# Convolution split by token halves, with gates and second-half taps inside the early attention

## The chip, the cores and the metric

The kernel runs on one core of one Trainium2 chip. The metric is the device time of one execution in microseconds; the median of three runs is given.

## What is computed

One layer of an encoder block on 1024 tokens with 1024 channels, in float32. Cut to what matters here:

```python
h = x @ w_in + b_in
h_conv = h[..., :1024]; q, k, v = ...          # 512 columns each, 8 heads of 64
g_conv, g_sb = sigmoid(h[..., 2560:3584]), sigmoid(h[..., 3584:4608])
# branch A
a, gate = split(h_conv)
c = a * sigmoid(gate)                           # 512 channels
c = causal_depthwise_conv(c, w_dw, width=31) + b_dw
y_conv = silu(layer_norm(c)) @ w_pw2 + b_pw2
# branch B, strictly causal, per head
z = q k^T / 8
att = exp(log_sigmoid(z) + suffix sums of log_sigmoid(-z))
y_sb = (att @ v) @ w_o
# both
mix = (g_conv * y_conv + g_sb * y_sb) @ w_out + b_out
x = layer_norm(alpha * x + mix)
# expert lookup: 8 heads, 16 of 16384 experts per head and token
y = peer(x)
out = layer_norm(alpha * x + y)
```

The 31 taps reach back 30 tokens, so the two halves of the tokens need only 30 columns of each other.

## The kernel before

The tokens are handled in reverse order, as two halves of 512. The "early" half is brought through attention, mixing and the first layer norm ahead of the expert lookup; attention and mixing of the "late" half run inside the lookup (all that has "late" in its name before the change). The diff touches only what lies ahead of the lookup.

Engines work from queues of their own, each in the order of its code, and wait for each other by semaphores. Stages, in the order of TensorE:

- *Projections.* A loop of four rounds (L601) with four weights a round, each weight 128 columns of `w_in` over all 1024 tokens: 48 matmuls in split precision (`split_products`, L206: high and low parts, three products, L209 to L211). A weight fills PSUM banks 2j and 2j+1, with j its place in the round, and waits until `psum_read[j]` says that the weight before it in these banks was read. The host orders the weights (L1622): conv tile c, its gate, q of c, k of c. ScalarE rounds each weight to its high part (L981), GpSimd subtracts to get the low one (L557, L562), in the memory of the weight; the next load of that place (L431) waits for the weight's matmuls. ScalarE makes the sigmoid of the gate (L1008) and evacuates q and k (L1012, L1016).
- *Convolution* on VectorE, tile by tile over both halves at once: gated input (L1322), 31 taps of 128x1024 (L1328, L1331), each waiting for the last one (`Steps.link`).
- *Values.* 8 blocks (`value_block`, L616), and between them mean and variance over channels as matmuls with a constant (L636, L643). VectorE centres and scales (L1341 to L1348), ScalarE does squares, root and swish (L1032 to L1038) and then evacuates the last four value blocks (L1026).
- *Attention*, 16 units n: four head pairs, and in each four query blocks with 512, 384, 256 and 128 keys. Per unit and head: scores (L662), sigmoids of both signs (L1051, L1054), the scan and the multiply on VectorE (L1356, L1360: the "stick"), transposes (L673), a copy (L1061), the product with the values (L685).
- *Gates and branches*, 8 steps m: weight m is rounded on ScalarE (L1084) and subtracted on VectorE (L1374), two gate groups of 24 matmuls (L712), the two branch products (L718), sigmoids (L1092) and `mix` on VectorE (L1382 to L1388).
- *The first output product* (L739) and its layer norm (L1418 on), queries, scores and the selection of experts, and then the lookup: 1024 gathers (L590), each with a dot product on VectorE (L1486).

## Time and profile before

| | |
|---|---|
| median of 3 runs | 3284.27 us (3281.8 to 3286.63) |
| profiled execution | 3283.15 us |
| its span | 3281.3 us |
| TensorE busy | 2446.8 us |
| VectorE busy | 2297.7 us |
| GpSimd busy | 1326.3 us |
| ScalarE busy | 1159.3 us |
| first matmul | 9.57 us |
| first output product ends | about 491.7 us |

The busy shares are means over stages with different limits. Ahead of the lookup the milestones are read from the order of time; in the lookup, from some 520 us on, the DMA engines are full. In rows, PE is TensorE's matmuls, PEld its weight loads, DVE VectorE, ACT ScalarE, POOL GpSimd. `arena_low` and `arena_high` are two overlays of the whole memory of a partition, so their names do not tell tiles apart; the line does.

### The profile page before, as it was taken

To read this page: it belongs to the slowest core of one execution; us is meant where nothing else is said; L and a number is where in the kernel's file an instruction comes from. 1 tells how busy PE (TensorE), PEld (TensorE's weight loads), DVE (VectorE), ACT (ScalarE), POOL (GpSimd) and SP (SyncE) were. 2 spreads that over 40 slices of the span, in tenths; PEclk is the share of its full clock that TensorE was granted. 3 is DMA by queue.
4 is the path that set the end of the run, shared out by engine and by line. 5 is a ranking of instruction groups with operands and counts; after the bars stand their busy time and mean duration, and the time that the engine had idled before them with its cause. 6 is when DMAs were issued, how large, how long until landed. Compare 5 with 4: busy or idle time off the path is not lost. (4 is left out here: it accounts for less than half of the span.)

```text
span 3281.3 us, 37294 instructions
## 1 busy us (share of the span) xinstructions
PE 2446.8 (75%) x12464; PEld 998.8 (30%) x12464; DVE 2297.7 (70%) x4704; ACT 1159.3 (35%) x3326; POOL 1326.3 (40%) x1197
## 2 busy tenths in 40 slices
PE   8987996778778777769899888885555555555555
PEld 7864653332223333323233332221111111111111
DVE  6986215776668888876667866666777677767775
ACT  3106112333334555533333333333333333333332
POOL 3400003344445544544343344444455445444553
PEclk9998997888888898889999999997777777777777
DMA  3101226999999999999999999999999999999997
GB/s 142 39 0 65 77 104 272 396 413 420 421 420 405 410 409 375 409 420 410 397 397 419 394 409 412 421 419 421 409 421 421 420 398 421 421 421 402 421 421 313
DMA packets 162792, 1163.71 MB, mean 355 GB/s; under 512 B 17857, under 2 KB 17985, under 8 KB 26178
## 3 DMA queue, kind: packets, MB, share of 16 engines
q0 software_dynamic: 147456, 1073.81, 79.7%
q1 hardware_dynamic: 15170, 87.79, 6.8%
q8 instruction: 93, 1.52, 0.2%
q14 instruction: 73, 0.60, 0.0%
HBM read 1157.33 MB, written 4.19 MB: 354 GB/s over the span
## 5 line engine op out<-in xcount | busy, mean ns | idle before, releaser
L809 PE MATMUL ps<-arena_high 64*64 64x512 f32 x8192 | 1275.3, 749 | 724.2 <-ACT arena_high L1163 721.2
L590 POOL DMA_INDIRECT arena_high<-uv_dram,idx_now x1024 | 1201.8, 1174 | 1468.7 <-PE ps L809 1269.4
L1486 DVE SCALAR_TENSOR_TENSOR arena_high<-arena_low,arena_high 128x1024 f32<-128x1024 f32 x1024 | 1237.2, 1224 | 631.4 <-DMA arena_high<-uv_dram,idx_now 620.8
L809 PEld LDWEIGHTS ps<-arena_high 64*64 64x64 f32 x8192 | 308.3, 156 | 1567.7 <-ACT arena_high L1163 1101.6
L1154 ACT ACTIVATE gcol<-hcol 128x2 f32<-128x2 f32 x512 | 103.7, 202 | 1405.8 <-DVE arena_high L1486 1403.7
L1163 ACT ACTIVATE arena_high<-arena_high,wcol 128x64 f32<-128x64 f32 x1024 | 300.4, 340 | 16.7
L1156 ACT ACTIVATE wcol<-gcol,arena_high 128x1 f32<-128x1 f32 x1024 | 245.7, 287 | 16.8
L778 PE MATMUL ps<-arena_low 128*128 128x512 f32 (+1 forms) x512 | 223.5, 580 | 0.0
L1331 DVE SCALAR_TENSOR_TENSOR arena_low<-arena_high,cols,arena_low 128x1024 f32<-128x1024 f32 x120 | 183.9, 1533 | 4.3
L585 POOL CAST idx_now<-arena_high 128x8 uint32<-128x8 f32 x128 | 59.0, 461 | 255.3 <-DVE arena_high L1472 254.7
L211 PE MATMUL ps<-x_hi_bytes,w_bytes 128*128 128x512 f32 x384 | 151.0, 393 | 0.0
L778 PEld LDWEIGHTS ps<-arena_low 128*128 128x128 f32 x512 | 93.9, 194 | 140.9 <-issue 124.3
L881 PE MATMUL ps<-arena_low 128*128 128x512 f32 x256 | 121.8, 620 | 0.0
L1154 ACT ACT_TABLE_LOAD x78 | 100.1, 1283 | 29.4 <-DVE arena_high L1486 28.1
L209 PE MATMUL ps<-x_hi_bytes,w_hi_bytes 128*128 128x512 f32 x256 | 100.8, 394 | 9.6 <-DVE x_lo_bytes L1312 9.6
L210 PE MATMUL ps<-x_lo_bytes,w_hi_bytes 128*128 128x512 f32 x256 | 100.6, 393 | 0.0
L1486 DVE DVE_READ_ACCUMULATOR arena_high<-arena_low,arena_high 128x1 f32 x1024 | 83.8, 82 | 0.0
L1148 ACT ACT_TABLE_LOAD x64 | 82.1, 1283 | 1.1
L211 PEld LDWEIGHTS ps<-x_hi_bytes,w_bytes 128*128 128x128 f32 x384 | 73.0, 190 | 15.5
L562 POOL TENSOR_TENSOR w_bytes<-arena_high,w_hi_bytes 128x1024 fp32r<-128x1024 f32 x12 | 34.8, 2906 | 91.0 <-ACT w_hi_bytes L981 90.9
L881 PEld LDWEIGHTS ps<-arena_low 128*128 128x128 f32 x256 | 47.7, 196 | 76.8 <-issue 76.7
L1522 DVE TENSOR_TENSOR_SCAN arena_low<-arena_low 128x1023 f32<-128x1023 f32 (+3 forms) x32 | 60.4, 1887 | 14.3 <-ACT arena_low L1194 13.9
(169 smaller groups left out, 2476.4 us busy)
## 6 DMA issues: line engine op xcount, KB each, us to landing
arena_low<-slabs_dram SPq DMA_DIRECT2D x21, 1152.0 KB
arena_high<-uv_dram,idx_now POOLq DMA_INDIRECT x1024
arena_high<-w_mix_dram SPq DMA_DIRECT2D x8, 1536.0 KB, 6.8
arena_low<-w_mix_dram SPq DMA_DIRECT2D x8, 1536.0 KB
arena_high<-w_proj_dram SPq DMA_DIRECT2D x16, 512.0 KB, 3.5
arena_high<-xT_dram SPq DMA_DIRECT2D x8, 512.0 KB, 7.7
arena_high<-w_out_dram SPq DMA_DIRECT2D x2, 2048.0 KB, 11.1
arena_high<-x_dram SPq DMA_DIRECT2D x8, 512.0 KB, 7.8
```

What stands on the lines that cost most here:

```text
L209: nc.tensor.matmul(out, w_hi, x_hi, start=first, stop=False)
L210: nc.tensor.matmul(out, w_hi, x_lo, start=False, stop=False)
L211: return nc.tensor.matmul(out, w_lo, x_hi, start=False, stop=last)
L590: pool.indirect_dma_start(out=ring[:, s % RING, :], out_offset=None, in_=uv_d, in_offset=bass.IndirectOffsetOnAxis(ap=idx_now[:, s:s + 1], ...
L778: last = nc.tensor.matmul(ps[:, 4 + half, j0 * P:j1 * P], w[:, k, half * P:(half + 1) * P], x1T[:, j0:j1, k, :], start=(k == 0), stop=(k = ...
L809: last = nc.tensor.matmul(ps[out_rows, bank, :], diag[rows, s % DIAGS, :], ring[rows, s % RING, cs], start=False, stop=False, skip_group_c ...
L881: last = nc.tensor.matmul(ps[:, 4 + g, :], w_mix_late[m % 2][:, o:o + P], xT_late[:, k, :], start=(k == 0), stop=(k == KD - 1))
L1154: steps.link(nc.scalar.activation(gcol[:, s0:s0 + 2], hcol[:, s0:s0 + 2], ACT.Gelu))
L1156: last = nc.scalar.activation(wcol[:, s:s + 1], gcol[:, s:s + 1], ACT.Copy, scale=gates[:, t % (BLK * PH), s:s + 1])
L1163: nc.scalar.activation(diag[:, s % DIAGS, :], ident64, ACT.Copy, scale=wcol[:, s:s + 1]).then_inc(diag_ready, 1)
L1331: ins = nc.vector.scalar_tensor_tensor(out=conv_both(c), in0=halves(conv_in[:, PAD - k:PAD - k + S]), scalar=cols[:, tap + k:tap + k + 1], ...
L1486: last = nc.vector.scalar_tensor_tensor(out=ring[:, s % RING, 0:D], in0=x1[c][:, j, :], scalar=1.0, in1=ring[:, s % RING, 0:D], op0=ALU.mu ...
```

## The change

- The host orders the weights: four pairs of conv tile and gate, then all q, then all k.
- The early half of the convolution is done by VectorE beside the projections, with taps of 128x512. The gated input of the late half is kept for all four tiles in `conv_in_late`. PSUM place 0 or 2 of a conv tile is read by VectorE, after the taps of the tile before.
- Statistics, centring and swish are done for each half apart: those of the early half between value blocks 0 and 3, those of the late half in the branch steps 1 to 4.
- The late half's 124 taps follow the early attention's multiplies, four behind each, and go by turns on two tiles, each waiting for the tap before it on its own tile.
- The gates: one of 16 groups of 24 matmuls per attention unit, ahead of the unit's transposes, with a sigmoid each. Their low parts are subtracted by GpSimd instead of VectorE, their weights are loaded apart from the branches' weights. Branch steps keep the branch products alone. Attention's scores have two PSUM banks instead of four.
- Some loads move: the first half of `w_out` comes when the gates are done, the second when the last mix is done; the x rows and bias rows come earlier.

The diff, cut to its core (moved addresses and new semaphores are left out):

```diff
@@ the queue of loads
+            sp_eng.wait_ge(proj_done, 4 * CC)
+            load_gate(0)
+            sp_eng.wait_ge(var_done, 1)
+            load_gate(1)
             sp_eng.wait_ge(v_done, NB)
...
+            for m in range(2, KD):
+                sp_eng.wait_ge(gates_done, 2 * m - 2)
+                load_gate(m)
...
+            sp_eng.wait_ge(mixed, KD)
             sp_eng.dma_start(w_out_early[1], w_out_d[:, CC:KD, :]).then_inc(wout_in[1], 16)
@@ GpSimd
+            def split_gates(m):
+                for g in range(2):
+                    gs = slice(g * D, (g + 1) * D)
+                    pool.wait_ge(w_rounded, m * 2 + g + 1)
+                    nc.gpsimd.tensor_tensor(w_lo_r[:, m % 2, gs], w_gate[:, m % 2, gs], w_hi_r[:, m % 2, gs].bitcast(F32),
+                                            ALU.subtract).then_inc(w_split, 1)
@@ TensorE
+            value_block(0)
+            pe.wait_ge(conv_done, CC)
+            conv_mean(1, 4)
+            value_block(1)
+            value_block(2)
+            conv_var(1, 5)
+            for b in range(3, NB):
                 value_block(b)
...
             scores_of(0)
             for n in range(NU):
+                gate_group(n)
+                turn_weights(n)
                 if n + 1 < NU:
                     scores_of(n + 1)
-                turn_weights(n)
...
             for m in range(KD):
...
+                if m == 1:
+                    pe.wait_ge(sigs_ready, 2 * KD)
+                    pe.wait_ge(conv_done, 2 * CC)
+                    conv_mean(0, 6)
+                if m == 3:
+                    conv_var(0, 7)
@@ ScalarE
+            for b in range(5, NB):
                 value_out(b)
+            round_w(1)
...
             for n in range(NU):
+                gate_sigmoid(n)
+                for hd in range(2):
+                    weights_out(n, hd)
                 for hd in range(2):
                     if n + 1 < NU:
                         stick_sigmoids(n + 1, hd)
-                    weights_out(n, hd)
+                if n % 2 == 1 and n // 2 + 2 < KD:
+                    round_w(n // 2 + 2)
@@ VectorE
             for c in range(CC):
+                a0, j = 4 * (c % 2) * HALF, 2 * (c % 2)
+                dve.wait_ge(proj_done, 2 * c + 1)
+                dve.wait_ge(psum_read[j + 1], START + c // 2 + 1)
+                if c >= 1:
+                    dve.wait_ge(conv_done, c)
...
+                nc.vector.scalar_tensor_tensor(out=conv_in_late[:, c, 0:HALF + PAD], in0=ps_flat[:, a0:a0 + HALF + PAD],
+                                               scalar=bias, in1=gate[:, 0:HALF + PAD], op0=ALU.add,
+                                               op1=ALU.mult).then_inc(psum_read[j], 1)
+                dve.wait_ge(psum_read[j], START + c // 2 + 1)
+                for k in range(TAPS):
+                    conv_tap(taps_done, c, 1, k)
...
             for n in range(NU):
                 for hd in range(2):
                     break_stick(n, hd)
+                    for i in range(4 * (2 * n + hd), 4 * (2 * n + hd + 1)):
+                        if i < CC * TAPS:
+                            pair, k = divmod(i, 2 * TAPS)
+                            late_tap(2 * pair + k % 2, k // 2)
@@ the host's order of the projection weights
 for c in range(CC):
-        order += [c * P, CONV + c * P, col_q + c * P, col_k + c * P]
+        order += [c * P, CONV + c * P]
+    order += [col_q + c * P for c in range(CC)] + [col_k + c * P for c in range(CC)]
```

How the order of instructions changes on VectorE in the second conv tile, beside the projections, before (`psum_read0`, `psum_read1` are places 0 and 1 of a round):

```order
L1322 SCALAR_TENSOR_TENSOR arena_high<-ps,cols,arena_high 128x1024 [waits conv_done,psum_read1,proj_done]
L1328 TENSOR_SCALAR arena_low<-arena_high,cols 128x2x512 [waits psum_read0]
L1331 SCALAR_TENSOR_TENSOR arena_low<-arena_high,cols,arena_low 128x2x512 [waits conv_step] x30
L1322 SCALAR_TENSOR_TENSOR arena_high<-ps,cols,arena_high 128x1024 [waits conv_done,psum_read1,proj_done]
L1328 TENSOR_SCALAR arena_low<-arena_high,cols 128x2x512 [waits psum_read0]
```

and now, from the second tile to the third:

```order
L1403 SCALAR_TENSOR_TENSOR arena_high<-ps,cols,arena_high 128x512 [waits conv_done,psum_read3,proj_done]
L1405 SCALAR_TENSOR_TENSOR arena_high<-ps,cols,arena_high 128x542
L1384 TENSOR_SCALAR arena_low<-arena_high,cols 128x512 [waits psum_read2]
L1387 SCALAR_TENSOR_TENSOR arena_low<-arena_high,cols,arena_low 128x512 [waits conv_step] x30
L1403 SCALAR_TENSOR_TENSOR arena_high<-ps,cols,arena_high 128x512 [waits conv_done,psum_read1,proj_done]
L1405 SCALAR_TENSOR_TENSOR arena_high<-ps,cols,arena_high 128x542
```

The tiles' PSUM reads alternate between places 0 and 2, and each stands behind 30 taps of half the width.

VectorE in attention, the first unit (512 keys), before:

```order
L1356 SCALAR_TENSOR_TENSOR arena_high<-arena_high,arena_low 128x511 [waits stick_zero,rest_done,starts_ready,normed]
L1360 TENSOR_TENSOR arena_high<-arena_high 128x512 [waits beta_done,stick_done]
L1356 SCALAR_TENSOR_TENSOR arena_high<-arena_high,arena_low 128x511 [waits rest_done]
L1360 TENSOR_TENSOR arena_high<-arena_high 128x512 [waits beta_done,stick_done]
L1356 SCALAR_TENSOR_TENSOR arena_high<-arena_high,arena_low 128x383 [waits rest_done]
```

and now, from its second head on (L1435 is the scan, L1439 the multiply):

```order
L1435 SCALAR_TENSOR_TENSOR arena_high<-arena_high 128x511 [waits rest_done]
L1439 TENSOR_TENSOR arena_high<-arena_high 128x512 [waits beta_done,stick_done]
L1454 SCALAR_TENSOR_TENSOR arena_low<-arena_high,cols,arena_low 128x512 [waits conv_late_step0]
L1454 SCALAR_TENSOR_TENSOR arena_low<-arena_high,cols,arena_low 128x512 [waits conv_late_step1]
L1454 SCALAR_TENSOR_TENSOR arena_low<-arena_high,cols,arena_low 128x512 [waits conv_late_step0]
L1454 SCALAR_TENSOR_TENSOR arena_low<-arena_high,cols,arena_low 128x512 [waits conv_late_step1]
L1435 SCALAR_TENSOR_TENSOR arena_high<-arena_high 128x383 [waits rest_done]
```

Four taps of two tiles by turns stand between a head's multiply and the next scan.

## Rows read from the trace of the kernel before

**Rows 1.** The page, busy tenths of the DMA engines in 40 slices.

```profile
DMA  3101226999999999999999999999999999999997
```

**Rows 2.** Stretches: start:end and length, busy us (instructions) per engine, PEclk, DMA.

```profile
196.00:206.00 10.00, 10.00 (x27) 6.55 (x26) 9.71 (x9) 0.23 (x1) 0.00 (x0) 0.66 0.01 2
...
291.00:303.00 12.00, 9.16 (x80) 5.39 (x76) 9.97 (x16) 9.08 (x25) 0.00 (x0) 1.00 0.00 1
...
344.00:380.00 36.00, 36.00 (x131) 24.33 (x130) 8.80 (x10) 6.84 (x9) 0.00 (x0) 1.00 0.24 88
```

**Rows 3.** ScalarE in order of time: start us, us, what, idle before.

```profile
34.32 1.28 ACT L1008 ACT_TABLE_LOAD   x1 [5.44 <-PE ps L211]
...
186.57 1.11 ACT L1016 ACTIVATE arena_low<-ps,cols 128x1024 f32<-128x1024 f32 x1 [9.76 <-PE ps L211]
```

**Rows 4.** VectorE in order of time, convolution and its norm.

```profile
36.95 1.28 DVE L1322 SCALAR_TENSOR_TENSOR arena_high<-ps,cols,arena_high 128x1024 f32<-128x1024 f32 x1 [18.92 <-ACT arena_high L1008]
...
90.02 0.81 DVE L1328 TENSOR_SCALAR arena_low<-arena_high,cols 128x1024 f32<-128x1024 f32 x1
90.87 49.82 DVE L1331 SCALAR_TENSOR_TENSOR arena_low<-arena_high,cols,arena_low 128x1024 f32<-128x1024 f32 x30
...
196.20 39.59 DVE L1331 SCALAR_TENSOR_TENSOR arena_low<-arena_high,cols,arena_low 128x1024 f32<-128x1024 f32 x30
...
260.94 6.55 DVE L1344 RECIPROCAL arena_high<-arena_high 128x1024 f32<-128x1024 f32 x1 [10.05 <-ACT arena_high L1034]
```

**Rows 5.** GpSimd's subtracts in order of time; VectorE's group of 59 to 66 us.

```profile
58.22 6.12 POOL L562 TENSOR_TENSOR w_bytes<-arena_high,w_hi_bytes 128x1024 fp32r<-128x1024 f32 x2 [8.48 <-ACT w_hi_bytes L981]
...
90.86 2.39 POOL L562 TENSOR_TENSOR w_bytes<-arena_high,w_hi_bytes 128x1024 fp32r<-128x1024 f32 x1 [7.34 <-ACT w_hi_bytes L981]
101.74 6.11 POOL L562 TENSOR_TENSOR w_bytes<-arena_high,w_hi_bytes 128x1024 fp32r<-128x1024 f32 x2 [8.50 <-ACT w_hi_bytes L981]
123.56 3.47 POOL L562 TENSOR_TENSOR w_bytes<-arena_high,w_hi_bytes 128x1024 fp32r<-128x1024 f32 x1 [15.71 <-ACT w_hi_bytes L981]
134.38 2.59 POOL L562 TENSOR_TENSOR w_bytes<-arena_high,w_hi_bytes 128x1024 fp32r<-128x1024 f32 x1 [7.35 <-ACT w_hi_bytes L981]
...
L1331 DVE SCALAR_TENSOR_TENSOR arena_low<-arena_high,cols,arena_low 128x1024 f32<-128x1024 f32 x3 | 7.9, 2631 | 0.1
```

**Rows 6.** TensorE in order of time, first values and first scores.

```profile
195.53 2.04 PE L620 MATMUL ps<-arena_high 1*128 1x512 f32 x2 [8.99 <-issue]
...
275.51 3.36 PE L662 MATMUL ps<-arena_low 64*128 64x512 f32 x8 [9.04 <-ACT arena_low L1026]
```

**Rows 7.** VectorE in order of time, a mix step.

```profile
351.07 0.75 DVE L1382 SCALAR_TENSOR_TENSOR arena_high<-ps,cols,arena_high 128x512 f32<-128x512 f32 x1 [16.47 <-PE ps L718]
351.74 0.68 DVE L1385 TENSOR_TENSOR arena_high<-ps,arena_high 128x512 f32<-128x512 f32 x1
```

**Rows 8.** Groups of the first 560 us, then two mix steps' starts.

```profile
L636 PE MATMUL ps<-arena_low,arena_high 128*128 128x512 f32 x16 | 7.0, 592 | 0.0
...
457.63 0.75 DVE L1382 SCALAR_TENSOR_TENSOR arena_high<-ps,cols,arena_high 128x512 f32<-128x512 f32 x1 [7.71 <-PE ps L718]
...
475.39 0.75 DVE L1382 SCALAR_TENSOR_TENSOR arena_high<-ps,cols,arena_high 128x512 f32<-128x512 f32 x1 [15.69 <-PE ps L718]
```

**Rows 9.** Attention's end in order of time: last multiply, last evacuation, rounding.

```profile
326.86 0.29 DVE L1360 TENSOR_TENSOR arena_high<-arena_high 128x128 f32<-128x128 f32 x1
...
328.39 0.60 ACT L1066 ACTIVATE arena_low<-ps 128x512 f32<-128x512 f32 x1 [0.54 <-PE ps L685]
328.88 3.89 ACT L1084 ACTIVATE w_bytes<-arena_high 128x1024 fp32r<-128x1024 f32 x4
```

**Rows 10.** Loads: weights from issue to landing; from 474 us on; output product's end.

```profile
arena_high<-w_proj_dram SPq DMA_DIRECT2D x16, 512.0 KB, 3.5
...
DMA to landing us min/median/max: 7.5/8.0/8.4
...
491.73 1.22 DVE L1418 SCALAR_TENSOR_TENSOR arena_high<-arena_high,ps 128x1024 f32<-128x1024 f32 x1 [14.18 <-PE ps L739]
```

More of the change, by code:

```diff
@@ L310, in build @@
         conv_step = sem("conv_step")
+        conv_late_step = [sem(f"conv_late_step{c}") for c in range(CC)]
         conv_done = sem("conv_done")
@@ L333, in build @@
         out_read = sem("out_read")
-        wmix_in = [sem(f"wmix_in{j}") for j in range(2)]
+        wgate_in = [sem(f"wgate_in{j}") for j in range(2)]
+        wbranch_in = [sem(f"wbranch_in{j}") for j in range(4)]
         gates_done = sem("gates_done")
@@ new lines, in _ @@
+            sp_eng.wait_ge(gates_done, 2 * KD)
+            sp_eng.dma_start(w_out_early[0], w_out_d[:, 0:CC, :]).then_inc(wout_in[0], 16)
+            sp_eng.wait_ge(av_done, NU)
+            load_branch(2)
+            load_branch(3)
+            sp_eng.dma_start(b_out_bc[0], b_out_d.partition_broadcast(P)).then_inc(rows_in, 16)
+            for m in range(4, KD):
+                sp_eng.wait_ge(branch_done, m - 3)
+                load_branch(m)
+            sp_eng.wait_ge(conv_done, 2 * CC)
@@ new lines, in _ @@
+            for it in range(2):
+                next_w1(it, 0)
+                gate_out(2 * it)
+                next_w1(it, 1)
+                next_w1(it, 2)
+                gate_out(2 * it + 1)
+                next_w1(it, 3)
+            for c in range(CC):
+                act.wait_ge(proj_done, 2 * CC + c + 1)
+                nc.scalar.activation(q_both(c), halves(ps_flat[:, 2 * c * HALF:(2 * c + 2) * HALF]), ACT.Identity,
+                                     bias=q_bias8[:, c:c + 1], scale=DH ** -0.5).then_inc(psum_read[c], 1)
+                next_w1(2, c)
@@ L1349, in _, with conv_tap @@
-            dve.wait_ge(normed, CC)
+            def conv_tap(steps, c, h, k):
+                tap = c * TAPS + C_CW + k
+                src = conv_in if h == 1 else conv_in_late[:, c, :]
+                src = src[:, PAD - k:PAD - k + HALF]
+                out = conv_h[h][:, c, :]
+                if k == 0:
+                    ins = nc.vector.tensor_scalar(out, src, cols[:, tap:tap + 1], cols[:, C_CB + c:C_CB + c + 1],
+                                                  ALU.mult, ALU.add)
+                else:
+                    ins = nc.vector.scalar_tensor_tensor(out=out, in0=src, scalar=cols[:, tap:tap + 1], in1=out,
+                                                         op0=ALU.mult, op1=ALU.add)
+                if k < TAPS - 1:
+                    steps.link(ins)
+                else:
+                    ins.then_inc(conv_done, 1)
@@ new lines, in conv_centre, with conv_scale @@
+            def conv_centre(h, bank):
+                dve.wait_ge(conv_done, CC * (2 - h))
+                dve.wait_ge(mean_done, 2 - h)
+                for c in range(CC):
+                    nc.vector.tensor_tensor(conv_h[h][:, c, :], conv_h[h][:, c, :], ps[:, bank, :],
+                                            ALU.subtract).then_inc(centred, 1)
+            def conv_scale(h):
+                dve.wait_ge(std_done, 2 - h)
+                nc.vector.reciprocal(rstd_row[h], rstd_row[h]).then_inc(rstd_done, 1)
+                dve.wait_ge(rstd_done, 2 - h)
+                dve.wait_ge(centred, CC * (2 - h))
+                for c in range(CC):
+                    nc.vector.tensor_tensor(conv_h[h][:, c, :], conv_h[h][:, c, :], rstd_row[h], ALU.mult).then_inc(normed, 1)
@@ L1352, in break_stick @@
+            conv_centre(1, 4)
+            conv_scale(1)
             def break_stick(n, hd):
```

312 lines of the change are left out of this document (147 added, 165 removed).

## The prediction

> **What bounds the kernel now.** I read the slices of the page first [rows 1]. From the seventh slice on (some 520 us) the DMA engines stand at 9 tenths: that is the expert lookup, fed by gathers, and it is the last 2760 us of the span. The diff touches nothing in it, so I let it move as one block: what the part before it gains or loses, the kernel gains or loses. That part is a chain of stages. TensorE leads it: 16 projection weights, 8 value blocks with the convolution's statistics, 16 attention units, 8 gate-and-branch steps, the first output product. The table of stretches [rows 2] shows where TensorE does not work: 9 us of silence before the values (it ends with the release called issue), 9 us before attention [rows 6], and about a quarter of attention itself; from 332 us to 475 us it never stops. VectorE is full only in the convolution, from 37 us to 236 us, beside the projections.
>
> The change can therefore win three things: half of the statistics' matmuls ahead of attention, the 9 us wait, and the idle quarter of attention. I price it by walking the new order from milestone to milestone.
>
> **Projections.** Matmuls come in steps: from the end of the 2nd weight (34.32) to that of the 16th (186.57) 14 weights take 10.88 us each [rows 3]. A weight's PSUM pair comes free when its reader is done. Before, VectorE's reader of a conv tile was wanted one round, 43.5 us, after the tile. Now all eight conv and gate weights come first, so a pair is used again after four weights, and the reader stands in VectorE's queue behind the taps of the tile before: the 9th weight (q of tile 0) waits for the third conv tile to be read, the 11th for the fourth.
>
> How fast do half-width taps go? A 1024-wide tap takes 1.285 us and starts every 1.32 (39.59 us for 30) [rows 4]. A 512-wide instruction of the same kind takes 0.75 [rows 7]; each early tap waits for the one before it, so with the same 0.04 it starts every 0.79. A tile is 30 x 0.79, 0.55 for the first tap (an estimate between half and all of the 0.81 of the full width) and 1.49 for the two instructions that read PSUM: 25.7 us.
>
> GpSimd is to be added. Its subtract for a projection weight falls among the taps, and a tap that meets one stands still: 2 of them in a row (58.22, 6.12 us) make 3 taps take 2.631 us each instead of 1.285, so 3 x 1.346 / 2 = 2.02 us a subtract [rows 5]. It checks out on whole tiles: the second tile takes 49.82 us for 30 taps instead of 39.59, with 5 subtracts in it [rows 4, 5]. A subtract follows its weight by about 4.6 us (3.5 to landing [rows 10], 1.05 to round). Tile 0 starts at 36.95 as before and meets 3 (39, 49, 60 us): it ends at 68.8. Tile 1 meets 3 (71, 82, 93): 100.6. Its successor is read by 102.1, and the 9th weight, due at 99.5, waits 2.7 us. Tile 2 meets 3 more (104, 118, 129): 132.4, and the last conv tile is read by 133.9. The 11th weight was due at 124.0: TensorE stands 10 us. After 9 us of silence before 195.5 us the granted clock was 0.66 in the next 10 us, its lower level for some 7 of them [rows 2]; I take 3.5 us for that here too. Then 134.0 + 6 x 10.88 + 3.5 = 202.8 for the end of the projections, against 186.5: **16.3 us late**. Both ends: 12.8 if the clock stays up, 18 if a subtract costs 2.2.
>
> **Values.** I keep the 9.0 us of silence behind the loop, since the loop and what follows it are the same code: start 211.8. Before, values and statistics took 195.5 to 266.5, with two groups of statistics of 7.0 us between them (mean and variance; one stands in [rows 8]); half of these go: 63.9 us, so 275.7. The early half's reciprocal (6.55 us at double width [rows 4]), centring and swish lie beside value blocks. ScalarE then evacuates the last value block (0.5), and now rounds gate weight 1 before attention (half of 3.89, so 2.0 [rows 9]), loads its table (1.28) and makes the first sigmoid (0.6): VectorE's first scan at 280.3, against 279.7. So the gain in front of attention, 15 us, pays for the loss in the projections and no more.
>
> **Attention with gates and taps.** VectorE now holds per unit its two sticks and eight taps. The sticks: 9.97 us busy in one of the four groups of four units [rows 2], and the others are alike; 41 us with the gaps between scan and multiply. The taps alternate between two tiles, so none waits for its neighbour; two such instructions start 0.67 apart though the first takes 0.75 [rows 7]. 124 x 0.67 = 83 us. To this comes GpSimd: 14 subtracts of gate weights of the same 1024 columns lie inside attention, the first ahead of the first scan, the second half over it: 1.3 + 12 x 2.03 = 25.7 us. Sum 150. The row does not show a scan or multiply of 512 under such a subtract; both read two SBUF tensors as the tap does, so I take the tap's toll. TensorE has 87 us of gates (16 groups of 24 at 10.88 / 48 = 0.227) and at full clock 4 x 9.2 = 37 of attention [rows 2]: 124, under 150, and between the last multiply of a unit and the next unit's sigmoid (transpose, scores, sigmoid: 2.0 us) VectorE has four taps, 2.7 us. So **VectorE becomes the bound**: 280.3 + 124.4 + 25.7 = 430.4. From its last multiply to the last evacuation was 1.84 us [rows 9]: branches start at 432.3.
>
> One rule of the Trainium skill speaks against the turns. VectorE: DVE Perf Modes, section The DRAIN you can't avoid, says that the next operation waits for the pipe to empty and that a semaphore between two operations costs nothing extra. By that rule alternating tiles buys nothing: +34.9 us in all instead of +20. [...]
>
> **Branches.** A gate-and-branch step takes 17.76 us (457.63 to 475.39 [rows 8]); 10.88 of it are gates, now gone: 8 x 6.88 = 55.0, and the late half's statistics, 7.0: 494.3. The last mix 2.1: 496.4. The first output product took 14.2 (477.5 to 491.7) [rows 10]. Its second weight half, 2 MB, is now asked for at its start and not 2 us earlier; such loads landed after 7.5 to 8.4 us, and it is wanted after 6.9: 1 us. End 511.6 against 491.7: **+20 us**. What follows on that queue (a bias row, the first slab) is less than before.
>
> **Other edits.** The gate loads (1 MB) have more than two units, some 18 us, to land, be rounded and subtracted; ScalarE, held at such a load behind its sigmoids, is next wanted a unit later. Cover gone, each late load would cost its 5 us. Bias rows and x load earlier, at nothing.
>
> **The rivals.** (1) *GpSimd's toll is less.* If half-width taps slip past a subtract, or it falls into gaps, both losses shrink at once. Without any toll the fourth conv tile is read at 115.7, before it is wanted; projections end at 186.5, VectorE ends attention at 388.5, the product at 468.5: 23 us faster, 3260. With x us a subtract the end moves by about 12.6x in attention and, above 0.6, by 9(x - 0.6) and the clock in the projections; it crosses zero near x = 1.2. Against it: 2.0 in [rows 5]; for it: no row has 512-wide taps. Chance 0.16, around 3279, half faster, half same. (2) *The silence behind the loop is swallowed* or the clock stays up in the projections: 9 or 3.5 us less, about 3294. For it: the page names no releaser for those 9 us. 0.10. (3) *The turns buy nothing*: a late tap starts 0.79 behind the last as an early one does, not 0.67, since the queue holds it anyway; 124 x 0.12 = 14.9 us more, 3319. Against it the 0.67 of [rows 7], for it that the 0.67 is of other operands. 0.08. (The page named above would have it so.) (4) *TensorE's clock falls in attention*, since it now waits for VectorE each unit: its 124 us grow past VectorE's 150 in places. A group of units with a quarter idle still had 1.00 [rows 2], and the values after 9 us of silence 0.66. Twice the time for a third of the units would be 0.33 x 124 = 41 us more, 165 in all against 150, less what VectorE's tolls overlap: some 8 us, 3312. 0.07. Forecast 0.59.
>
> **The numbers.** The profiled execution took 3283.15 (span 3281.3), 1.1 under the median of 3284.27. 3283.15 + 19.9 = 3303; with the median's 1.1, 3304. Its own range, from 12.8 or 18 in the projections and 22 to 29 in attention, is 3297 to 3310. For 8 in 10 I go down to 3288, which takes in rival 2 and the dearer part of rival 1, and up to 3318. A measurement of this kernel tells about 0.2%, 6.6 us, from no change. Faster 0.08, same 0.08, slower 0.84.
>
> **What would show it.** In the profile after: the second conv weight round must show TensorE idle about 3 and 10 us near 100 and 124 us, released by VectorE's PSUM read; projections end near 203; the first scan comes near 280; in attention VectorE is busy over 90% with taps of 0.75 us and 2.8 us where a subtract meets them, and TensorE waits each unit for the multiply; gathers begin some 20 us later. If TensorE never stands in the projections, or taps never stretch, rival 1 is true. If attention lasts under 130 us, I am wrong on what bounds it.

## The result, and the profile after

The changed kernel took 3301.16 us (median of 6 runs, 3291.51 to 3304.47) against 3285.77 (6 runs, 3281.8 to 3288.72): 1.0042 times the kernel before, with an interval of 1.0026 to 1.0058. The forecast was 3304, in a range of 3288 to 3318. The profiled execution took 3303.23, its span is 3301.4 against 3281.3.

The lookup differs by some microseconds from execution to execution, though no kernel here changes it: from the first gather to the end the traces show 2757 to 2769 us. So I read the stages ahead of it by milestones and end at the first gather: 523.22 before, 539.93 after, 16.7 us later. The other 3.4 of the 20.1 between the two spans are in the lookup, and the medians differ by 15.4.

| milestone (us from the span's start) | before | forecast | after |
|---|---|---|---|
| TensorE goes on behind the read of the third conv tile; its wait | none | 102.1, 2.7 | 100.4, 1.2 |
| the same for the fourth; its wait | none | 134.0, 10 | 132.6, 10.1 |
| last k evacuated from | 186.6 | 202.8 | 200.5 |
| values start | 195.5 | 211.8 | 201.8 |
| first scan | 279.7 | 280.3 | 270.2 |
| last multiply of attention ends | 327.2 | 430.4 | 425.0 |
| output product read | 491.7 | 511.6 | 508.5 |
| first gather | 523.2 | (+20) | 539.9 (+16.7) |

TensorE after, in order of time, only rows with a wait (start, length, what, idle before and its releaser); they answer to [rows 6]:

```profile
100.35 0.50 PE L210 MATMUL ps<-x_hi_bytes,w_hi_bytes 128*128 128x512 f32 x1 [1.24 <-DVE arena_high L1405]
...
132.55 0.77 PE L210 MATMUL ps<-x_hi_bytes,w_hi_bytes 128*128 128x512 f32 x1 [10.10 <-DVE arena_high L1405]
...
201.78 1.38 PE L649 MATMUL ps<-arena_high 1*128 1x512 f32 x2 [1.30 <-ACT arena_low L1070]
...
318.95 1.12 PE L705 MATMUL ps<-arena_high 128*128 128x128 f32 x4 [5.16 <-DVE arena_high L1439]
```

The first two are the waits that the new weight order makes, L1405 being VectorE's read of a conv tile. The third is the surprise, the start of the values: 1.30 us of idle time where [rows 6] had 8.99. The fourth stands for four of their kind, of 3.4 to 5.2 us: TensorE waits for VectorE's multiply.

Stretches after (start:end, length, busy us of TensorE, its weight loads, VectorE, ScalarE and GpSimd, then the granted clock), answering to [rows 2]:

```profile
132.00:142.00 10.00, 9.45 (x31) 7.64 (x32) 9.54 (x14) 0.00 (x0) 0.00 (x0) 0.72 0.00 0
...
201.00:211.00 10.00, 9.22 (x24) 6.54 (x25) 0.00 (x0) 2.64 (x3) 4.43 (x2) 0.66 0.31 107
291.00:303.00 12.00, 12.00 (x66) 9.69 (x65) 11.93 (x15) 3.92 (x9) 5.19 (x2) 1.00 0.11 45
318.00:328.00 10.00, 9.05 (x31) 6.20 (x32) 9.24 (x15) 2.24 (x5) 0.00 (x0) 0.66 0.00 0
```

In 291:303 VectorE (third pair of numbers) was busy 9.97 of 12 us before and is busy 11.93 now: it is full. Behind the 10 us wait the clock shows 0.72 for 10 us, behind the wait of 5.16 us 0.66, and at the start of the values, behind idle time of 1.30 us, 0.66 too; the last comes back in experiment 5.

VectorE after, in order of time, and GpSimd's subtract beside it:

```profile
270.18 2.92 DVE L1435 TENSOR_TENSOR_SCAN arena_high<-arena_high 128x511 f32<-128x511 f32 x1 [31.50 <-ACT arena_high L1119]
...
417.69 0.43 DVE L1439 TENSOR_TENSOR arena_high<-arena_high 128x256 f32<-128x256 f32 x1
418.03 2.74 DVE L1454 SCALAR_TENSOR_TENSOR arena_low<-arena_high,cols,arena_low 128x512 f32<-128x512 f32 x4
...
424.67 0.29 DVE L1439 TENSOR_TENSOR arena_high<-arena_high 128x128 f32<-128x128 f32 x1
```

```profile
267.27 4.76 POOL L596 TENSOR_TENSOR w_bytes<-arena_high,w_hi_bytes 128x1024 fp32r<-128x1024 f32 x2 [0.87 <-ACT w_hi_bytes L1076]
```

Four taps take 2.74 us alone, 0.67 from start to start. The first scan took 2.92 us and not the 1.22 of its undisturbed kind, since GpSimd's two subtracts (267.3 to 272.0) lie over it.

### The profile page after: what moved, and what is told of

It is laid out like the page before. It is cut to its first block and busy times, and to the rows that moved or that the text cites. A ratio compares the mean times of both kernels' runs of the same rounds, so it can differ in the third digit from the quotient of the medians.

```text
span 3301.4 us, 37453 instructions
## 1 busy us (share of the span) xinstructions
PE 2441.4 (74%) x12464; PEld 1002.3 (30%) x12464; DVE 2312.8 (70%) x4825; ACT 1165.8 (35%) x3337; POOL 1368.7 (41%) x1213
## 5 line engine op out<-in xcount | busy, mean ns | idle before, releaser
L619 POOL DMA_INDIRECT arena_high<-uv_dram,idx_now x1024 | 1217.8, 1189 | 1457.2 <-PE ps L852 1256.2
L852 PE MATMUL ps<-arena_high 64*64 64x512 f32 x8192 | 1260.8, 742 | 740.1 <-ACT arena_high L1222 736.9
L1222 ACT ACTIVATE arena_high<-arena_high,wcol 128x64 f32<-128x64 f32 x1024 | 300.5, 340 | 16.7
L1215 ACT ACTIVATE wcol<-gcol,arena_high 128x1 f32<-128x1 f32 x1024 | 245.7, 287 | 16.8
L210 PE MATMUL ps<-x_hi_bytes,w_hi_bytes 128*128 128x512 f32 x384 | 156.7, 408 | 20.6 <-DVE arena_high L1405 11.3
L211 PE MATMUL ps<-x_lo_bytes,w_hi_bytes 128*128 128x512 f32 x384 | 153.8, 401 | 0.0
L821 PEld LDWEIGHTS ps<-arena_low 128*128 128x128 f32 x512 | 93.8, 193 | 139.7 <-issue 122.7
L1387 DVE SCALAR_TENSOR_TENSOR arena_low<-arena_high,cols,arena_low 128x512 f32<-128x512 f32 x120 | 110.9, 924 | 4.3
L1454 DVE SCALAR_TENSOR_TENSOR arena_low<-arena_high,cols,arena_low 128x512 f32<-128x512 f32 x120 | 103.3, 921 | 0.0
L210 PEld LDWEIGHTS ps<-x_hi_bytes,w_hi_bytes 128*128 128x128 f32 x384 | 75.0, 195 | 41.5 <-issue 24.4
L211 PEld LDWEIGHTS ps<-x_lo_bytes,w_hi_bytes 128*128 128x128 f32 x384 | 75.1, 195 | 15.3
```

The source lines that it names most:

```text
L210: nc.tensor.matmul(out, w_hi, x_hi, start=first, stop=False)
L211: nc.tensor.matmul(out, w_hi, x_lo, start=False, stop=False)
L619: pool.indirect_dma_start(out=ring[:, s % RING, :], out_offset=None, in_=uv_d, in_offset=bass.IndirectOffsetOnAxis(ap=idx_now[:, s:s + 1], ...
L821: last = nc.tensor.matmul(ps[:, 4 + half, j0 * P:j1 * P], w[:, k, half * P:(half + 1) * P], x1T[:, j0:j1, k, :], start=(k == 0), stop=(k = ...
L852: last = nc.tensor.matmul(ps[out_rows, bank, :], diag[rows, s % DIAGS, :], ring[rows, s % RING, cs], start=False, stop=False, skip_group_c ...
L1215: last = nc.scalar.activation(wcol[:, s:s + 1], gcol[:, s:s + 1], ACT.Copy, scale=gates[:, t % (BLK * PH), s:s + 1])
```

## Experiments

The traces before and after left three questions: where the 9 us of silence ahead of the values went; whether it is GpSimd that makes attention 155 us long; and whether VectorE's taps need to be in attention at all.

### 1. Is the silence ahead of the values the loop, or VectorE?

The kernel before with 23 of 31 taps in a tile, so its result is not the one asked for; nothing of the loop over the weights changes.

```diff
-                for k in range(1, TAPS):
+                for k in range(1, TAPS - 8):
```

> The kernel before, with 23 instead of 31 full-width taps on each conv tile (the last 8 taps of each tile are left out, so this run's convolution is shorter than asked). It asks what the 9 us of TensorE's silence ahead of the first value block were, which the forecast took for something behind the loop that any kernel keeps. Theory 1: the first value block waits for all four PSUM places, and place 0 was read for the last time by VectorE's fourth conv tile, at 194.04 + 1.28 = 195.3 in the trace of before. With 8 taps of 1.32 us less on three tiles (31.7 us) that read comes once its projection and gate are done, at about 168, and TensorE starts the values about 1.3 us after the last projection, at 188, with no release by issue of 9 us. Rival: the silence belongs to the end of the loop (code, registers): it stays 9 us and the values start at 195.5. The convolution ends near 195 instead of 236, so nothing else in front of attention should get later; the time is some 7 us under the kernel before by theory 1 and the same within noise by the rival.

TensorE's first value matmul there, and in the kernel before VectorE's read of the fourth conv tile:

```profile
187.43 1.09 PE L620 MATMUL ps<-arena_high 1*128 1x512 f32 x2 [1.30 <-ACT arena_low L1016]
```

```profile
194.04 1.28 DVE L1322 SCALAR_TENSOR_TENSOR arena_high<-ps,cols,arena_high 128x1024 f32<-128x1024 f32 x1
```

The silence is gone with the same loop: values start at 187.4, 1.3 us behind the last projection. Before, the fourth conv tile is read at 194.04 to 195.32 and the values start at 195.53, since TensorE waits for all four PSUM places ahead of the first value block, and one of them was VectorE's. The first scan came at 269.7, 10 us earlier than before, and the first gather at 513.96, 9.3 earlier. The one time, 3282.35 against a median of 3285.07, shows only part of that: this execution's lookup was 2767 us long, the one before's 2758.

### 2. What does the weight order cost?

The changed kernel with q weights set between the conv tiles, so that no PSUM place is wanted again before its reader is done; everything else, attention too, is unchanged.

```diff
+WEIGHTS = [("A", 0), ("G", 0), ("A", 1), ("G", 1), ("Q", 0), ("Q", 1), ("A", 2), ("G", 2),
+           ("Q", 2), ("Q", 3), ("A", 3), ("G", 3), ("K", 0), ("K", 1), ("K", 2), ("K", 3)]
```

> The changed kernel with the projection weights in another order: conv and gate of tiles 0 and 1, q 0 and 1, conv and gate of tile 2, q 2 and 3, conv and gate of tile 3, k 0 to 3. Nothing else but the order of ScalarE's readers that goes with it. Theory: the two waits of TensorE in the projections (1.2 and 10.1 us, with a lower clock after the second) come from PSUM places whose reader stands behind the taps of the tile before; here the place is wanted a round later. VectorE's reads come at 36.6, 68.5, 100.3 and some 147, and no weight waits: projections end at 186.5 instead of 200.5. The early taps end at 173 instead of 159, the value weight is rounded after them and split by 188, so the values start near 188 to 190 instead of 201.8, and the whole is 11 to 14 us faster than the changed kernel: 3287 to 3290. Rival: the taps' end is what the values really wait for (the value weight's high part lies where the convolution's input lies), so the values start after 190 and the gain is under 5 us.

It took 3286.05 (10 runs), 0.9999 times the kernel before (0.9985 to 1.0012). Its trace:

```profile
132.00:142.00 10.00, 10.00 (x46) 8.29 (x45) 0.00 (x0) 1.21 (x2) 2.40 (x1) 1.00 0.17 52
...
252.00:406.00 154.00, 129.24 (x652) 95.22 (x651) 148.17 (x188) 56.58 (x123) 32.19 (x13) 0.91 0.13 42
```

```profile
186.63 1.09 PE L658 MATMUL ps<-arena_high 1*128 1x512 f32 x2 [1.30 <-ACT arena_low L1068]
```

No wait in the projections, values at 186.6, first scan at 251.9 (18 us earlier than after: 15 at the start of the values, 3 by the clock behind it), first gather at 520.8 (19 earlier). Attention is as long as after, 154.2 us with VectorE busy for 148 of them. So the order alone costs 15 us of the median, and even without it the rest of the change gains nothing: the first scan is 28 us earlier than before and what follows attention 81 us shorter, but attention is 107 us longer (154.2 for 47.5).

### 3. Do the turns on two tiles help?

The second-half taps tile by tile, each waiting for the one before.

```diff
-                            pair, k = divmod(i, 2 * TAPS)
-                            late_tap(2 * pair + k % 2, k // 2)
+                            late_tap(*divmod(i, TAPS))
```

> The changed kernel with the late taps one tile after the other instead of by turns on two: each late tap waits for the one right before it. Theory: a dependent tap starts 0.79 us after the last (as the early taps do), an independent one 0.66 to 0.67, so 124 taps cost 0.12 x 124 = 15 us more. Not all of it shows, since VectorE waited for ScalarE at the heads of wide units (0.3 to 0.7 us each, some 6 us in all): 9 to 15 us slower than the changed kernel. The rule of the Trainium skill, page VectorE: DVE Perf Modes, section The DRAIN you can't avoid, by which a semaphore between two operations costs nothing extra, gives 0.

3310.47 (4 runs), 1.0073 (1.0051 to 1.0095): 9.3 us over the changed kernel. Four taps behind a multiply, here:

```profile
339.95 3.11 DVE L1454 SCALAR_TENSOR_TENSOR arena_low<-arena_high,cols,arena_low 128x512 f32<-128x512 f32 x4
342.97 0.42 DVE L1435 TENSOR_TENSOR_SCAN arena_high<-arena_high 128x127 f32<-128x127 f32 x1
```

3.02 us from the first tap to the scan, against 2.65 for the same with turns: 0.79 from start to start where a tap waits for its neighbour, 0.67 where not. Attention takes 163.1 us, 8.3 more than after. Rival 3 of the prediction falls, and its price of 14.9 was high: only three of four taps follow a tap, 31 x 0.37 = 11.5, and the waits for ScalarE in attention shrank from 5.0 us to 3.5.

### 4. Is it GpSimd that fills attention?

The changed kernel without the 16 subtracts of gate weights on GpSimd; TensorE takes the high part in the low part's place, with as many matmuls, so the low part is missing from the result.

```diff
-                    nc.gpsimd.tensor_tensor(w_lo_r[:, m % 2, gs], w_gate[:, m % 2, gs], w_hi_r[:, m % 2, gs].bitcast(F32),
-                                            ALU.subtract).then_inc(w_split, 1)
+                    pool.sem_inc(w_split, 1)
```

> The changed kernel without GpSimd's 16 subtracts of the gate weights; the third product of a gate takes the high part of the weight instead of the low part, which is left out of the computation. Matmuls, loads and all else are as they are. Theory of the toll: each of 12 to 13 subtracts inside attention holds VectorE for 2.03 us; attention (first scan to last multiply, 154.8 us in the changed kernel) falls by 24 to 26 us, and by the lower clock behind the toll's waits too, to 126 to 131, near TensorE's own 124, and the time to about 3273 to 3277. Rival: attention is held by the chain from multiply to next sigmoid over TensorE, and VectorE's toll falls into slack: it falls by less than 10 us, and taps wait for ScalarE instead.

3266.8 (4 runs), 0.9935 (0.9914 to 0.9955), 34 us under the changed kernel, where I had expected 24 to 28; 30 of them are attention, 3 the clock at the start of the values (experiment 5). VectorE's groups from the first scan to the last multiply, after, and in this kernel (count | busy us, mean ns | idle before, releaser; the 31.5 us ahead of the first scan are in it):

```profile
L1454 DVE SCALAR_TENSOR_TENSOR arena_low<-arena_high,cols,arena_low 128x512 f32<-128x512 f32 x120 | 103.3, 921 | 0.0
L1435 DVE TENSOR_TENSOR_SCAN arena_high<-arena_high 128x511 f32<-128x511 f32 (+3 forms) x32 | 27.8, 870 | 36.7 <-ACT arena_high L1119 36.5
L1439 DVE TENSOR_TENSOR arena_high<-arena_high 128x512 f32<-128x512 f32 (+3 forms) x32 | 19.9, 622 | 1.1
```

```profile
L1453 DVE SCALAR_TENSOR_TENSOR arena_low<-arena_high,cols,arena_low 128x512 f32<-128x512 f32 x120 | 82.1, 745 | 0.0
L1434 DVE TENSOR_TENSOR_SCAN arena_high<-arena_high 128x511 f32<-128x511 f32 (+3 forms) x32 | 26.1, 816 | 34.1 <-ACT arena_high L1118 34.1
L1438 DVE TENSOR_TENSOR arena_high<-arena_high 128x512 f32<-128x512 f32 (+3 forms) x32 | 15.7, 492 | 1.1
```

The toll is 21.2 us on the taps, 1.7 on the first scan and 4.2 on multiplies: 27 in all, in 14 subtracts. VectorE's busy time falls from 148.5 to 120.8 us, attention from 154.8 to 124.7, and TensorE's clock is 1.00 in two stretches of 33 us (303 to 369) where it was 0.90.

### 5. The same subtracts on VectorE

14 of the 16, one behind every second unit's taps.

```diff
-            for m in range(1, KD):
-                split_gates(m)
...
+                    if n % 2 == 0 and n < 2 * KD - 2:
+                        gate_split(n // 2 + 1, hd)
```

> The changed kernel with 14 of the 16 gate subtracts (all but gate weight 0) put on VectorE, one behind every second unit's taps, instead of on GpSimd; nothing else moves. What is asked: is it GpSimd's subtract that lengthens VectorE's work in attention, or only one more thing beside it? Theory (a subtract on GpSimd takes 2.0 to 2.2 us from VectorE): the changed kernel's attention of 154.8 us holds 12 to 14 tolls; instead of each stands a 1024-wide instruction of about 1.15 us of VectorE's own. Attention 155 - 14 x 2.1 + 14 x 1.15 = 142 us, the first gather 12 us earlier, near 527, time near 3289. Rival (attention is set by TensorE, whose clock falls to half after each wait, with 124 us of work at full clock): the length stays within 3 us of 155, the time near 3301. A second rival: VectorE's own subtract stands in line ahead of a unit's scan and ScalarE's rounding arrives late for it; then attention is longer than now, 160 us and more, 3306 and up.

3281.35 (10 runs), 0.9986 (0.9977 to 0.9996): 20 us under the changed kernel, where I had expected 12.

```profile
L1463 DVE TENSOR_TENSOR w_bytes<-arena_high,w_hi_bytes 128x1024 fp32r<-128x1024 f32 x14 | 17.1, 1220 | 0.3 <-ACT w_hi_bytes L1074 0.3
```

```profile
L1433 DVE TENSOR_TENSOR_SCAN arena_high<-arena_high 128x511 f32<-128x511 f32 (+3 forms) x32 | 26.1, 816 | 31.5 <-ACT arena_high L1117 31.5
```

A subtract costs VectorE 1.22 us when it does it, and 2 when GpSimd does it. Attention is 138.0 us, 16.8 shorter. VectorE's busy time in it fell by 12 (148.5 to 136.6), 10 of them the tolls less its own subtracts (27 - 17). The other 5 us are idle time: VectorE waits for ScalarE nowhere in attention any more, since the 31.5 us lie ahead of the first scan, where it was 36.5.

Some 5 us more lie ahead of the first scan, which came at 265.4 for 270.2: 1.7 of them up to the start of the values, and 3.1 in the values. These 3.1 are no gain of this kernel. Here and in experiments 2, 3 and 4 the first scan comes 65.2 us behind the start of the values, after 68.4, though TensorE's idle time ahead of the values is 1.3 us in all of them. The granted clock differs, 0.91 over these 20 us in the changed kernel and 1.00 in experiment 4:

```profile
186.00:206.00 20.00, 18.70 (x73) 14.27 (x73) 0.00 (x0) 2.80 (x3) 0.00 (x0) 0.91 0.15 53
```

```profile
186.00:206.00 20.00, 18.70 (x80) 14.56 (x80) 0.00 (x0) 2.74 (x3) 0.00 (x0) 1.00 0.15 53
```

TensorE is busy for 18.70 us in both, with 73 matmuls in the one and 80 in the other. Why the clock fell in the one execution and not in the others stays open.

### 6 and 7. The taps ahead of attention

If VectorE bounds attention and idles ahead of it (after, its busy time from 206 to 270 us was 8.3 of 64 us), the taps belong there. First with the order of experiment 2: 16 of the second-half taps behind the third conv tile's early taps, 36 behind the fourth's, 24 between centring and scaling, 48 behind the scaling.

```diff
+                if c in {2: 16, 3: 36}:
+                    late_some({2: 16, 3: 36}[c])
...
             conv_centre(1, 4)
+            late_some(24)
             conv_scale(1)
+            late_some(48)
```

> The kernel with the other weight order (conv tile and gate weights spread, the last conv tile's weights just ahead of the k weights) and with all 124 second-half taps ahead of attention: 16 behind the third tile's early taps, 36 behind the fourth's, 24 between centring and scaling, 48 behind the scaling. The work is the same, only VectorE's order is another. That weight order alone measured 3286.05 with the first scan at 251.9, attention of 153.9 us and the first gather at 520.8. Theory (VectorE sets the length of attention; what idles on it ahead of attention is free): the 48 last taps end near 253, the first scan comes within 2 us of 252, attention falls to what TensorE needs, 124 to 128 us as without the subtracts (124.5), the first gather comes 26 to 29 us earlier, near 493, time 3257 to 3260, faster than the kernel before by 0.8%. Rival 1 (GpSimd's subtracts hold scans and multiplies on the path from unit to unit, with no taps to hold): attention near 140, time 3272. Rival 2 (gates in attention starve TensorE anyway): no more than 5 us gained, 3281 and up.

3261.75 (5 runs), 0.9934 (0.9921 to 0.9948). Attention fell to 119.6 us, but the first scan came at 261 and not at 252. GpSimd, VectorE and TensorE of that place:

```profile
247.54 0.42 POOL L610 MEMSET arena_high<- 128x384 f32 x1 [39.88 <-PE ps L221]
247.90 12.90 POOL L611 COPY arena_high<-arena_high 128x128 f32<-128x128 f32 x1
```

```profile
228.75 31.90 DVE L1418 SCALAR_TENSOR_TENSOR arena_low<-arena_high,cols,arena_low 128x512 f32<-128x512 f32 x48
260.96 3.29 DVE L1480 TENSOR_TENSOR_SCAN arena_high<-arena_high 128x511 f32<-128x511 f32 x1 [0.31 <-POOL arena_high L611]
```

```profile
267.00 1.12 PE L714 MATMUL ps<-arena_high 128*128 128x128 f32 x4 [11.91 <-DVE arena_high L1484]
```

A copy of 128 columns, 0.29 us elsewhere, lasts 12.9 us on GpSimd, until VectorE's row of 48 taps ends; the scan needs its result. Here VectorE holds GpSimd up, the other way round than in [rows 5].

Then with the changed kernel's own weight order: 72 taps behind the fourth tile's, 20 and 32 around the scaling.

```diff
+                if c in {3: 72}:
+                    late_some({3: 72}[c])
```

> The changed kernel with its own weight order, and the 124 second-half taps ahead of attention: 72 behind the fourth tile's early taps, 20 between centring and scaling, 32 behind the scaling. It tells how much of the change's loss lies in taps inside attention and how much in the weight order. Theory: projections and first scan as in the changed kernel (201 and 270, at most 3 later since 72 taps and the x and weight subtracts beside them end near 217, centring began at 215), attention 124 to 128 instead of 154.8, first gather near 512, time near 3273; so the weight order alone costs e6_taps_ahead against this 13 to 18 us. Rival 1 (subtracts on the path from unit to unit): attention near 140, 3287. Rival 2 (the taps slow the projections' and values' PSUM readers): the first scan at 275 and later.

3276.28 (10 runs), 0.9960 (0.9944 to 0.9975). The time is 3 us above my 3273, but by another sum: attention is 117.2 us, shorter than the 124 I expected, and the first scan 279.9, 10 later. The same reversal shows, at a place that costs more:

```profile
160.57 40.08 POOL L584 TENSOR_TENSOR w_bytes<-arena_high,w_hi_bytes 128x1024 fp32r<-128x1024 f32 x1 [8.08 <-ACT w_hi_bytes L1025]
```

```profile
200.71 0.80 PE L210 MATMUL ps<-x_hi_bytes,w_hi_bytes 128*128 128x512 f32 x1 [12.51 <-POOL w_bytes L584]
```

The last projection weight's subtract, 2.4 us otherwise, took 40 beside a row of taps (158.6 to 198.4), and TensorE stood 12.5 us.

### 8 and 9. Who holds whom

Two kernels test it: experiment 6 with 24 of the last 48 taps moved into attention, one to a stick, so that VectorE is free when the copy comes; and experiment 7 with each tap linked to the one before.

```diff
-            late_some(48)
+            late_some(24)
...
                     break_stick(n, hd)
+                    if n >= 4:
+                        late_some(1)
```

> As e6_taps_ahead, but of the 48 taps behind the scaling 24 stay there and the last 24 follow the sticks inside attention, one each from the fifth unit on. In e6_taps_ahead the 48 ran without a gap from 228.75 to 260.6, GpSimd's small copy of the starts (0.29 us elsewhere) lasted from 247.90 to 260.8 beside them, and the first scan waited for it until 260.96; TensorE idled 12 us behind it. Theory (a row of taps with no wait between them keeps GpSimd out until it ends): with 24 the row ends near 245, before the copy is due; the copy takes 0.3 us, the first scan comes at 252 to 253, 8 to 9 us earlier; attention, set by TensorE with 119 us in e6_taps_ahead, has VectorE free for more than half of the time, so 24 single taps (16 us) hide: 120 to 124. First gather near 490, time 3253 to 3256. Rival (the copy was late by GpSimd's own delay or by ScalarE's rounding; the taps inside attention cost their time): the scan stays near 260, attention grows by 10 to 16 us, time 3262 to 3275.

3252.88 (5 runs), 0.9901 (0.9883 to 0.9918): 1% faster than the kernel before and 48 us under the changed one.

```profile
247.92 0.29 POOL L611 COPY arena_high<-arena_high 128x128 f32<-128x128 f32 x1
```

```profile
252.07 2.92 DVE L1480 TENSOR_TENSOR_SCAN arena_high<-arena_high 128x511 f32<-128x511 f32 x1 [7.09 <-ACT arena_high L1131]
```

```profile
248.00:268.00 20.00, 17.86 (x94) 13.02 (x95) 9.75 (x11) 11.44 (x22) 5.04 (x5) 1.00 0.26 85
270.00:370.00 100.00, 100.00 (x564) 76.46 (x563) 60.29 (x76) 47.63 (x106) 29.67 (x12) 1.00 0.16 53
```

The copy takes 0.29 us, the scan comes at 252.1, and in attention TensorE is busy 100 of 100 us at full clock, VectorE 60, GpSimd 30: the tolls are still paid, in time that nobody waits for. Attention is 116.5 us.

```diff
-                    pair, k = divmod(next(taken), 2 * TAPS)
-                    late_tap(2 * pair + k % 2, k // 2)
+                    late_tap(*divmod(next(taken), TAPS))
```

> As e7_taps_ahead_same_order, but the second-half taps go tile by tile, so each waits for the one before it, in place of by turns on two tiles. In e7_taps_ahead_same_order 60 taps without a wait between them ran from 158.6 to 198.4, GpSimd's subtract of the last projection weight lasted 40.08 us beside them (160.57 to 200.65; 2.4 elsewhere), and TensorE waited for it 12.5 us, to 200.71. Theory (VectorE keeps GpSimd out for as long as its instructions follow without a wait; a wait of 0.1 us lets it in): the last projection subtract takes 2.4 to 5 us, TensorE does not wait near 200, values start at 201.8 as in the changed kernel and not at 214.6; the taps cost 0.79 each and the row of 72 ends past 217, near 225. Rival (GpSimd is slowed by the amount of VectorE's traffic, not by the lack of a wait): the subtract takes 30 us and more here too, and TensorE waits.

```profile
162.55 2.59 POOL L584 TENSOR_TENSOR w_bytes<-arena_high,w_hi_bytes 128x1024 fp32r<-128x1024 f32 x1 [8.55 <-ACT w_hi_bytes L1025]
```

```profile
159.76 32.92 DVE L1406 SCALAR_TENSOR_TENSOR arena_low<-arena_high,cols,arena_low 128x512 f32<-128x512 f32 x30
```

With a wait of 0.04 us between taps (start to start 0.79, the instruction 0.75) the subtract gets through in 2.59 us for 40.08, TensorE does not wait, values start at 202.5 for 214.6. The taps pay instead: 30 take 32.9 us where 30 x 0.79 = 23.7 were due, since they now meet that subtract and eight half as wide behind it. The two kernels end alike (first gather 514.5 and 514.1; 3280.45 in one run), since the slower row ends at 281 and now holds the first scan, which would have been due near 273. The 124 taps are the same in both and only their order and the waits between them differ, so in this pair it is not the amount of VectorE's traffic that keeps GpSimd out. There is one trace of each, and a row without waits does not always do so (what stays open, below).

## Why the prediction was right, and where it was not

**What bounds the kernel: right.** The table of stages moved as one chain. From the output product's end to the first gather are 31.5 us before and 31.4 after, and the lookup added nothing beyond its scatter.

**Projections: right, 2.3 us too dear.** The two waits came where they were put, 1.2 and 10.1 us for 2.7 and 10. Three early tiles took 29.6 to 29.9 us for 30 taps with the subtracts in them, as in the sum (29.8); but VectorE's first instruction of the convolution came at 35.1 us and not at 36.95, which brings 1.5 us at the fourth tile, and the clock behind the second wait cost 2.7 us and not 3.5.

**The silence behind the loop: wrong, 7.7 us.** The failed step is "I keep the 9.0 us of silence behind the loop, since the loop and what follows it are the same code". It took a label, issue, for a cause. Experiment 1 shows the cause: the fourth conv tile, still unread by VectorE. In the changed kernel that reader is done by 133 us, and 1.3 us remain. Part of what rival 2 described therefore happened, at a chance of 0.10, and its reason stood in the prediction ("the page names no releaser"). The trace of before had it: VectorE's reader L1322 ends at 195.32, 0.2 us before TensorE starts. With 10 us off, 202 came out instead of 212 for the start of values, and 270 instead of 280 for the first scan.

**Values: 63.9 us, right by luck.** The 63.9 were taken from values that started behind 9 us of silence, at a clock of 0.66. Without the silence that loss should have gone too, and in experiments 2 to 5 it did (3.2 us less to the first scan). The profiled execution of the changed kernel showed the 0.66 all the same, behind 1.30 us.

**Attention: the mechanism right, 4.7 us too cheap.** VectorE is the bound, without tolls it needs what was said (124.4 forecast, 124.7 in experiment 4), and the toll of a subtract is 2 us as in [rows 5]. Mis-sized were the 25.7 us for the tolls, and their effects were put at nothing. Experiment 4 gives 27 us of tolls. Beyond these VectorE waited for ScalarE at eight more unit heads, 5.0 us in all (36.5 less the 31.5 ahead of the first scan), in experiment 4 at three, 2.6 us, in experiment 5 at none. The order of time suggests how: where two subtracts hold VectorE, TensorE waits for the multiply (3.4 to 5.2 us), its clock falls behind that (the 0.66 above), and the next sigmoid is late. That is rival 4's mechanism in small, at some 3 to 5 us and not 8; what the clock alone adds was not tested.

The Trainium skill, page SBUF — State Buffer, section Who interferes with whom, says that VectorE with two SBUF inputs and GpSimd reading SBUF exclude each other for a whole instruction, and that issue order decides who blocks. The traces agree that they exclude each other: VectorE lost 2.0 us a subtract in experiment 4. The 38 us that GpSimd lost in experiment 7 go beyond one instruction, and no sentence there covers them.

**Branches and the output product: 2.4 us too cheap.** From attention's last multiply to the product's reader are 83.6 us, forecast 81.2. The last evacuation ended 4.0 us behind that multiply and not 1.8, and the product's wait is 15.1 us against 14.2 in [rows 10], the 1 us that was put there for the late half of its weight (not tested alone).

**The sum.** -2.3, -7.7, +4.7 and +2.4 make -2.9: 508.7 for the forecast 511.6, and 508.5 was measured. Errors of opposite sign, not good numbers all through, brought the total within 3 us. Had the silence been read right and nothing else, the forecast would have been 3296, and 3293 with the clock that goes with it. Two small slips in the sums do not carry the outcome: 41 and 83 make some 124.1, not 124.4, and rival 1's end of the product, 388.5 plus 81.2, is 469.7 and not 468.5.

**Against the rivals.** Rival 1 (less toll) fell in experiment 4, rival 3 (turns buy nothing) in experiment 3: they buy 9 us. The rule cited beside it from the Trainium skill, VectorE: DVE Perf Modes, section The DRAIN you can't avoid, that a semaphore between two operations costs nothing extra, isn't what these traces show (0.79 us from start to start with a wait, 0.67 without). The same section says besides that a next operation that is not held starts earlier, and with that the 0.67 agrees; the prediction read the page too narrowly there.

What stays open is when a row of taps without waits keeps GpSimd out. In the changed kernel's own attention it does not:

```profile
310.21 5.62 POOL L596 TENSOR_TENSOR w_bytes<-arena_high,w_hi_bytes 128x1024 fp32r<-128x1024 f32 x2 [10.41 <-ACT w_hi_bytes L1076]
```

The first of the two was issued 0.13 us into the first of four such taps, ran behind it, and the second took turns with the next tap, each of the two taps between lasting 2.8 to 2.9 us. In experiment 6 eight 512-wide subtracts did the same from 171.70 us on, the first issued in the second tap of its row (each tap 1.77 for 0.75). Those that stayed out until the row ended, six in experiments 6 to 8, were issued when five or more such instructions had begun. No run tests whether that is the rule.

## What to carry to other kernels

Move work to an engine not by how busy it is over the span but by the stage in which it idles: 100 of the 124 taps moved from attention to the time beside projections and values made the kernel 33 us faster (experiment 8 against 2, 3252.9 for 3286.05), since attention, where the same change had also put GpSimd's subtracts and TensorE's gates, was where VectorE was full. Where a wait is labelled issue and the code there waits for several semaphores, look on every engine for what ended within 0.2 us before the waiting instruction. VectorE and GpSimd instructions that both read two tensors from SBUF nearly add up as if on one engine (2.0 of a subtract's 2.4 us), so where VectorE is the bound give them to whichever costs it less (1.22 us for 2.0 here), and put no long unbroken row on VectorE while something that others wait for stands in GpSimd's queue.

## What the hardware showed that I had not expected

- A long row of VectorE instructions without waits can keep GpSimd out until it ends: 40.08 us for a 128x1024 subtract that takes 2.4 (experiment 7), 12.90 for a copy that takes 0.29 (experiment 6). With each linked to the last, 2.59 (experiment 9). Subtracts issued in the first or second instruction of such a row got in.
- While VectorE's instruction reads one tensor from PSUM and one from SBUF, GpSimd's subtract runs beside it: in experiment 6 four of them (202.98, 0.6 us apart) kept their pace, and the subtract held up before them ended at 205.30, 2.2 us behind the last tap of the row: it ran beside them.
- TensorE's granted clock was 0.72 over 10 us after a wait of 10.1 us and 0.66 after one of 5.16. After one of 1.24 us it was 1.00; after 1.30 us ahead of the values it was 0.66 in the changed kernel's trace, 1.00 in experiments 2 to 5, and 0.83 in experiments 1 and 9.
